# Experts' weights in 4 MB transfers from the eleventh expert on, normed tokens in the gathers' order, and memory products beside every second expert

## The reference

```python
def routed_experts(h, w_router, b_router, w_gate_up, b_gate_up, w_down, b_down):   # top 4 of 32
    ...
    def expert_block(args):
        xb, e = args
        gu = xb @ w_gate_up[e] + b_gate_up[e]          # (1024 x 2048)
        g, u = gu[:, :D_EXPERT], gu[:, D_EXPERT:]
        g = jnp.minimum(g, SWIGLU_LIMIT)
        u = jnp.clip(u, -SWIGLU_LIMIT, SWIGLU_LIMIT)
        glu = g * jax.nn.sigmoid(SWIGLU_ALPHA * g)
        return ((u + 1.0) * glu) @ w_down[e] + b_down[e]   # (1024 x 1024)
```

## Time and profile before

| | |
|---|---|
| median of three runs | 1755.46 us |
| the profiled execution: time, span | 1756.94 us, 1755.1 us |
| busy share PE, PEld, DVE, ACT, POOL | 93%, 59%, 40%, 33%, 1% |
| moved from HBM | 544 MB, mean 311 GB/s over the span |
| chain that ended last | PE 48%, DMA 31% (w_down 28%, w_gate_up 2%) |
| L948, gate_up's matmuls | 2000 records, 445.2 us busy |
| L989, down's matmuls | 992 records, 228.2 us busy |
| issues of w_gate_up, w_down | 125 and 61 of 2048 KB, 22.1 and 21.3 us to landing |
| issues of mem_w_kv | 8 of 1024 KB, 16.9 us to landing |

### The profile page before, as it was taken

One profiled execution on the slowest core, in us unless ns is written; L12 is line 12 of the kernel. 1 busy time (PEld: TensorE's weight loads), 2 busy tenths in 40 slices (PEclk: granted clock), 3 DMA queues, 4 the chain that ended last, 5 costly groups with the idle time before them and its releaser, 6 DMA issues.

```text
span 1755.1 us, 20263 instructions
## 1 busy us (share of the span) xinstructions
PE 1638.5 (93%) x8849; PEld 1033.2 (59%) x8850; DVE 705.3 (40%) x875; ACT 572.7 (33%) x787; POOL 22.5 (1%) x37
## 2 busy tenths in 40 slices
PE   8999999798889999998888888899999999999998
PEld 7788533333334444532323232378888998988886
DVE  5897412111111211211111111177664865567653
ACT  6576200111011111100000011176554765455552
POOL 0000000000000000000000000010000000000000
PEclk9999899999999999999999999999999999999999
DMA  7538999999999999999999999956555523445552
GB/s 246 174 101 307 382 427 428 427 427 427 427 428 426 428 427 427 427 427 427 429 428 428 427 426 427 408 169 208 188 191 174 170 97 126 165 135 187 191 192 96
DMA packets 118763, 546.39 MB, mean 311 GB/s; under 512 B 5697, under 2 KB 64193, under 8 KB 92977
## 3 DMA queue, kind: packets, MB, share of 16 engines
q1 hardware_dynamic: 117344, 540.96, 77.4%
q0 software_dynamic: 1040, 4.00, 0.8%
q10 hardware_dynamic: 288, 0.11, 0.0%
HBM read 544.00 MB, written 1.05 MB: 311 GB/s over the span
## 4 chain that ended last, share of the span: by engine, by line
PE 48%; DMA 31%; ACT 1%; DVE 1%; issue 0%; DVEq 0%; ACTq 0%
DMA ring<-in_w_down 28%; PE PS L624 8%; PE PS L989 8%; PE PS L1146 6%; PE PS L626 4%; PE PS L948 3%; DMA ring<-in_w_gate_up 2%; PE PS L609 1%; PE PS L610 1%; PE PS L611 1%; PE PS L1161 1%; DMA ring<-in_w_ple_gate 1%; PE PS L576 1%; PE PS L578 1%; PE PS L577 1%; PE PS L662 1%
## 5 line engine op out<-in xcount | busy, mean ns | idle before, releaser
L948 PE MATMUL PS<-ring,work 128*64 128x512 f32 x2000 | 445.2, 597 | 32.6 <-DMA ring<-in_w_gate_up 32.6
L1967 DVE TENSOR_TENSOR ring<-ring,ring 128x2048 fp32r<-128x2048 f32 (+2 forms) x130 | 289.3, 2234 | 258.6 <-ACT ring L1388 258.5
L948 PEld LDWEIGHTS PS<-ring,work 128*64 128x64 f32 x2000 | 138.8, 137 | 319.2 <-issue 246.9
L1388 ACT CAST ring<-ring 128x2048 fp32r<-128x2048 f32 (+2 forms) x131 | 243.2, 1869 | 211.4 <-DMA ring<-in_mem_w_kv 85.4
L989 PE MATMUL PS<-ring,work 128*64 128x512 f32 x992 | 228.2, 603 | 53.3 <-DMA ring<-in_w_down 40.4
L989 PEld LDWEIGHTS PS<-ring,work 128*64 128x64 f32 x992 | 71.9, 138 | 195.7 <-issue 152.5
L2399 DVE TENSOR_SCALAR work<-PS 128x512 f32<-128x512 f32 x32 | 22.1, 690 | 319.6 <-PE PS L948 319.6
L1643 ACT ACTIVATE work<-work 128x512 f32<-128x512 f32 x32 | 20.2, 631 | 361.0 <-DVE work L2399 361.0
L2295 DVE TENSOR_TENSOR work<-PS,work 128x512 fp32r<-128x512 f32 x32 | 22.1, 692 | 248.8 <-ACT work L1587 248.8
L624 PE MATMUL PS<-work,ring 128*128 128x512 f32 x320 | 111.2, 392 | 0.0
L624 PE MATMUL PS<-ring 128*128 128x512 f32 x320 | 111.2, 394 | 0.0
(11 more groups left out here) (437 smaller groups left out, 2332.9 us busy)
## 6 DMA issues: line engine op xcount, KB each, us to landing
ring<-in_w_gate_up SPq DMA_DIRECT2D x125, 2048.0 KB, 22.1
ring<-in_w_down SPq DMA_DIRECT2D x61, 2048.0 KB, 21.3
ring<-in_ffn_w_gu SPq DMA_DIRECT2D x44, 1024.0 KB, 5.1
ring<-in_w_in SPq DMA_DIRECT2D x28, 1024.0 KB, 5.5
ring<-in_ffn_w_down SPq DMA_DIRECT2D x22, 1024.0 KB, 4.7
ring<-in_w_out SPq DMA_DIRECT2D x8, 1024.0 KB, 5.1
ring<-in_mem_w_kv SPq DMA_DIRECT2D x8, 1024.0 KB, 16.9
work<-in_w_gate_up SPq DMA_DIRECT2D x2, 2048.0 KB, 18.7
```

What stands on the lines that cost most here:

```text
L948: t = e.matmul(PS[hf * 64:hf * 64 + 64, bank, :], XG[g % 2][:, 2 * kp + kk, i * 64:(i + 1) * 64], raw_chunk(w, kk)[:, c0 + hf * 512:c0 + h ...
L1388: e.copy(hi(j), raw(j)).then_inc(*act.now(("hi", j)))
L1967: e.tensor_tensor(lo(j), raw(j), hi(j).bitcast(F32), ALU.subtract).then_inc(*dve.now(("lo", j)))
```

## The change

The experts' two matrices may be joined from expert 10 on (up to 29): two parts in one transfer of 4 MB into two neighbouring slots. For that the two parts must be neighbours in memory on each partition: with rows `(p k)`, four rows of w_gate_up per partition in each half (32 KB) and all eight of w_down (32 KB); a single part takes two or four of them. The features of the tokens follow: `hnh` and `hnl` are written in the order in which the gathers read them, by reading x with a stride of four, so that a gather's weights are contiguous; `g_ffn_pairs` is permuted on the host. The hidden values follow as well: each half of the array now takes four of eight hidden columns in turn (`hidden`), for the weights and for the biases. The memory products move from experts 11 to 18 to every second one from 11 to 25, the transpose of p from 26 to 27, POOL's loads of p and the masks from group 5 to group 7. ACT's norm of the memory vectors also waits for DVE's `crowded`. The branch `spilled` follows the new row order.

```diff
--- before.py
+++ after.py
@@ -88,10 +88,10 @@
 PACKED = ("mem_w_kv_2", "w_ple_proj")
 X, Y, APART = NS, NS + 1, NS + 2
 CHECK = 6
-JOINED, FIRST_JOINED = (), 99
+JOINED, FIRST_JOINED = ('w_gate_up', 'w_down'), 10
 MEM_T = (6, 7, 9, 10)
-MEM_KV = tuple(range(11, 19))
-P_T, PLE_PROJ = 26, (28, 29, 30, 31)
+MEM_KV = tuple(range(11, 27, 2))
+P_T, PLE_PROJ = 27, (28, 29, 30, 31)
 
 
 class Plan:
@@ -118,7 +118,7 @@
             if e < NE:
                 add(("gate_up", e), [("w_gate_up", 2 * k, 2, 0, 2048) for k in range(4)], e, False)
             if e in MEM_KV:
-                add(("beside", e), [("mem_w_kv_2", 0, 8, (e - MEM_KV[0]) * 256, 256)])
+                add(("beside", e), [("mem_w_kv_2", 0, 8, MEM_KV.index(e) * 256, 256)])
             if e in PLE_PROJ:
                 add(("beside", e), [("w_ple_proj", 0, 2, (e - PLE_PROJ[0]) * 256, 256)])
             if e:
@@ -422,6 +422,11 @@
         hT32 = W(18240, 8, 256)
         hnl, hnh, rn = R32(0, 2, D), R32(2048, 2, D), ss_of["out"]
         XG = [W(4096, 8, 256), W(6144, 8, 256)]
+
+        def by_rows(v):
+
+            return v.rearrange("p (a q k) -> p a k q", a=2, k=4)
+
         PGr, PGr4 = R32(8192, 2, 256), R32(8192, 2, 4, 64)
         PGb = [B16(8704 + 512 * i, 2, 4, 128) for i in range(2)]
         PW = [R32(9728 + 256 * i, 256) for i in range(2)]
@@ -859,12 +864,15 @@
                 t = logits(k)
             t.then_inc(*pe.now("logits"))
 
+            def hidden(v, hf):
+                return v.rearrange("p (q z r) -> p q z r", z=2, r=4)[:, :, hf, :]
+
             def biases(n):
 
                 one_e = selb[0:96, n:n + 1].to_broadcast([96, 64])
                 for bank, c0 in ((bank_g(n), 0), (bank_u(n), DE)):
                     for hf in range(2):
-                        e.matmul(PS[hf * 64:hf * 64 + 64, bank, :], one_e, bgub[0:96, c0 + hf * 512:c0 + hf * 512 + 512],
+                        e.matmul(PS[hf * 64:hf * 64 + 64, bank, :], one_e, hidden(bgub[0:96, c0:c0 + DE], hf),
                                  start=True, stop=False, skip_group_check=True)
 
             for i in range(4):
@@ -887,7 +895,7 @@
                         if c == 0:
                             e.wait_ge(*dve["PG", g, h])
                         for z, half in enumerate((hnh, hnl)):
-                            t = e.matmul(PS[:, bank, c * 256:(c + 1) * 256], half[:, h, 256 * i + c:256 * i + 256:2],
+                            t = e.matmul(PS[:, bank, c * 256:(c + 1) * 256], half[:, h, 256 * i + c * 128:256 * i + c * 128 + 128],
                                          PGr[:, h, :], start=h == 0 and z == 0, stop=h == 1 and z == 1, skip_group_check=True)
                 t.then_inc(*pe.now(("gather", g, i)))
 
@@ -947,7 +955,7 @@
                             for hf in range(2):
                                 t = e.matmul(PS[hf * 64:hf * 64 + 64, bank, :],
                                              XG[g % 2][:, 2 * kp + kk, i * 64:(i + 1) * 64],
-                                             raw_chunk(w, kk)[:, c0 + hf * 512:c0 + hf * 512 + 512], start=False,
+                                             hidden(raw_chunk(w, kk)[:, c0:c0 + DE], hf), start=False,
                                              stop=kp == 3 and kk == 1, skip_group_check=True)
                     t.then_inc(*pe.now(("w", w), *([("gu", n)] if kp == 3 else [])))
 
@@ -1020,7 +1028,7 @@
                 e.wait_ge(o_bias, 16)
                 e.transpose(PS[:, 5, 0:16], obr, ident[0:16, 0:16]).then_inc(o_pe, 1)
                 for j in range(8):
-                    e.wait_ge(o_dma[j % 2], 32 * (j // 2 + 1))
+                    e.wait_ge(o_dma[j % 2], 64 * (j // 2 + 1))
                     e.wait_ge(o_v, 2 + 5 * j)
                     for i in range(2):
                         for k in range(8):
@@ -1029,7 +1037,7 @@
                     m.then_inc(o_pe, 1)
                 e.wait_ge(o_v, 2 + 5 * 8)
                 for j in range(4):
-                    e.wait_ge(o_dma[j % 2], 128 + 16 * (j // 2 + 1))
+                    e.wait_ge(o_dma[j % 2], 256 + 16 * (j // 2 + 1))
                     for kk in range(2):
                         for h in range(2):
                             for nb in range(2):
@@ -1571,7 +1579,8 @@
             x_chunks(2)
             e.wait_ge(*dve["factor_out"])
             for h in range(2):
-                e.activation(hnh[:, h, :], x[:, h, :], ACT.Identity, scale=rn[:, h:h + 1]).then_inc(*act.now(("hnh", h)))
+                e.activation(hnh[:, h, :].rearrange("p (a k q) -> p a k q", a=2, k=4), by_rows(x[:, h, :]), ACT.Identity,
+                             scale=rn[:, h:h + 1]).then_inc(*act.now(("hnh", h)))
             e.wait_ge(*dve["nmx"])
             for h in range(2):
                 e.activation(coef[:, h, :], lgx[:, h, 0:32], ACT.Exp, bias=nmx[:, h:h + 1]).then_inc(*act.now(("coef", h)))
@@ -1606,6 +1615,7 @@
             def memory_norm(h):
 
                 e.wait_ge(mem_in, 16 * (h + 1))
+                e.wait_ge(*dve["crowded"])
                 e.activation(mem_sq, mem, ACT.Square, accum_out=ss_of["mem_s"][:, h:h + 1]).then_inc(*act.now(("sq_mem_s", h)))
                 root("mem_s", h, ss_of["mem_s"])
 
@@ -1620,7 +1630,7 @@
                                          ACT.Identity, scale=gain("mem_kv_norm_2", k))
                     t.then_inc(*act.now(("beside", n)))
                 elif n in MEM_KV:
-                    c = n - MEM_KV[0]
+                    c = MEM_KV.index(n)
                     e.wait_ge(*pe["beside", n])
                     o = kT[:, 2 * c:2 * c + 2, :] if c < 4 else vm[:, :, (c - 4) * 256:(c - 3) * 256]
                     e.copy(o, PS[:, BM, :].rearrange("p (c t) -> p c t", c=2)).then_inc(*act.now(("beside", n)))
@@ -2245,9 +2255,11 @@
             def normed_rest(h, part):
 
                 c0, c1 = ((0, 256), (256, 512), (512, D))[part]
+                k0, k1 = ((0, 2), (2, 4), (0, 4))[part]
                 e.wait_ge(*act["hnh", h])
-                e.scalar_tensor_tensor(out=hnl[:, h, c0:c1], in0=x[:, h, c0:c1], scalar=rn[:, h:h + 1],
-                                       in1=hnh[:, h, c0:c1].bitcast(F32), op0=ALU.mult,
+                e.scalar_tensor_tensor(out=hnl[:, h, c0:c1].rearrange("p (k q) -> p k q", q=128),
+                                       in0=by_rows(x[:, h, :])[:, c0 // 512, k0:k1, :], scalar=rn[:, h:h + 1],
+                                       in1=hnh[:, h, c0:c1].bitcast(F32).rearrange("p (k q) -> p k q", q=128), op0=ALU.mult,
                                        op1=ALU.subtract).then_inc(*dve.now(("hnl", h, part)))
 
             normed_rest(0, 0)
@@ -2327,7 +2339,7 @@
                     e.wait_ge(o_turned, 1)
                     for c in range(8):
                         t = e.tensor_scalar(hT32[:, c, :], PS[:, 4 + c // 2, (c % 2) * 256:(c % 2) * 256 + 256],
-                                            gain("g_ffn", c), None, ALU.mult)
+                                            gain("g_ffn_pairs", c), None, ALU.mult)
                     t.then_inc(o_normed, 1)
                     with e.Fori(0, NE) as n:
                         m = e.value_load(cnt[0:1, bass.ds(n, 1)], min_val=0, max_val=S)
@@ -2795,7 +2807,7 @@
                     t = e.tensor_copy(PGb[g % 2][:, h, :, :].rearrange("p i (z s) -> p i z s", z=2),
                                       bc(PGr4[:, h, :, :].bitcast(F32), [128, 4, 2, 64], 2))
                 t.then_inc(*pool.now(("PGb", g)))
-                if g == 5:
+                if g == NE // 4 - 1:
                     e.wait_ge(*pe["beside", MEM_KV[-1]])
                     e.dma_start(p_raw, d["p"].rearrange("(h p) n -> p h n", p=128)).then_inc(p_in, 16)
                     e.dma_start(cst[:, C_HM:C_N], d["cst"][:, C_HM:C_N]).then_inc(hm_in, 16)
@@ -2825,9 +2837,10 @@
                     elif p.expert < 0:
                         src = rows(w, p.k0, p.k, p.c0, p.n)
                     elif p.name == "w_gate_up":
-                        src = w[p.expert][p.k0 * 128:(p.k0 + p.k) * 128, :].rearrange("(p k) n -> p k n", p=128)
+                        r0, k0 = p.k0 // 4 * 512, p.k0 % 4
+                        src = w[p.expert][r0:r0 + 512, :].rearrange("(p k) n -> p k n", p=128)[:, k0:k0 + n * p.k, :]
                     else:
-                        src = w[p.expert][p.k0 * 128:(p.k0 + p.k) * 128, :].rearrange("(p k) n -> p k n", p=128)
+                        src = w[p.expert].rearrange("(p k) n -> p k n", p=128)[:, p.k0:p.k0 + n * p.k, :]
                     if j == plan.apart:
                         e.wait_ge(*pe["merged_t", 3])
                         for kk in range(2):
@@ -2861,7 +2874,9 @@
                         e.wait_ge(o_pe, 1 + j - 1)
                     for i in range(2):
                         src = d["w_gate_up"][bass.ds(n, 1), :, i * DE + j * 128:i * DE + j * 128 + 128]
```

(6 more changed lines are left out.)

## The result

The changed kernel takes **1785.41 us** (median of 5 runs, 1780.68 to 1788.92) beside 1755.66 of the kernel before (5 runs, 1755.32 to 1760.34): a ratio of 1.0164, 95% interval 1.0153 to 1.0176. That is 29.8 us slower. I had forecast 18.5 slower, 1774.0, and a range up to 1781. The side and the mechanism were right. The size was not: the stream's start was priced too low, and losses that I had put at nothing were there. The profiled execution has a span of 1783.6 us, 28.5 more than before.

A forecast was written before the change was run, and what follows sets the result against it. The experts' in-order weight stream was taken to bound the kernel. Five gaps (23.7 us) less the joins' saving (5.5) plus the tokens' new order (0.3) made +18.5 on 1755.46: 1774.0 us, range 1754 to 1781.

The forecast's parts named there:

- the stream's start: Start and completion of a transfer issued into an empty stream: 2.1 us, 2.5 in the middle, from lone 1024 KB loads.
- What bounds: Experts' stage: the in-order weight stream decides, not the engines; a stretch in which it runs dry is lost for good.
- What a joined transfer saves: Weight stream: 0.107 us per 4096 KB transfer, 5.5 us for 51 joined ones (0 to 10.9).
- Rival B: Stream gaps as forecast, but a 4096 KB transfer saves nothing: dry 23.2 us, 1779.0 us; chance 11%.
- The setup-cost rule: Trainium skill: roughly fixed 2 us per transfer, 102 us for 51 if paid in the stream; forecast: full queue hides it.
- Where it goes dry: Loads of experts 14, 18, 20, 22, 26, whose second gate_up pair waits for memory weights' slots; nothing lost at 11, 15, 23.
- How large a gap is: Each dry place behind a memory product: 9.65 + 2.67 + 2.1 - 9.68 = 4.74 us, five are 23.7.
- The clock: PE idles about 5.3 us ahead of down, its clock falls to 0.50, down's first half takes 2.67 us more, all five places.
- Rival A: Gaps are there but the clock holds: 5 x 2.07 = 10.4 us, so 1760.7 us; chance 20%.
- The later stages: Everything after the experts' stage: unchanged, only later.
- The front: Normed tokens' strided reads on ACT and DVE before the experts' stream: 0.3 us, between 0 and 2.2.
- The sum: Whole kernel: 23.7 - 5.5 + 0.3 = +18.5 us, onto the median 1755.46: 1774.0 us; forecast's chance 42%.

The follow-up runs named there:

- experiment 1: Changed kernel with no joined transfers, everything else of the change kept: 1757.77 us, ratio 1.0006 to the kernel before.
- experiment 4: Changed kernel, both kinds joined, with PE making the memory product ahead of down's first half instead of between the halves: 1756.78 us, ratio 1.0000.
- experiment 2: Changed kernel with only w_gate_up joined (35 transfers), w_down as singles: 1756.07 us, ratio 0.9995.
- experiment 5: Changed kernel plus overwritten bf16 matmuls in PE's idle time ahead of down: 1781.52 us with 40 of them, 1780.30 us with 84.
- experiment 8: Changed kernel with the memory products beside experts 11 to 18 again, both kinds joined (55 joined loads): 1786.62 us, ratio 1.0164.
- the second run of experiment 5: Changed kernel plus a row of 84 overwritten bf16 matmuls, in place of 40, in PE's idle time ahead of down: 1780.30 us, ratio 1.0136.

## Where the prediction failed, and what it had right

In the span I forecast 18.5 us more, and it was 28.5. Two steps failed. The start of a stream that has stopped was priced at 2.1 us and took 3.1 on average. And everything outside five places behind memory products was put at nothing ("the whole after the experts' stage unchanged, only later"), but three more late loads cost 4.2, PE's late end 1.8 and a later stage 2.0. The saving was 1.9 too large on top of that. Smaller terms took 1.9 of all this back. Term by term:

- **What bounds**: right. The stream's dry time is the loss; experiment 1, with all but the joins, has none, and experiment 4, with all joins and no dry step behind a memory product, has no loss that can be measured.
- **What a joined transfer saves**: forecast 0.107, measured 0.07. In the changed kernel PE's waits for w_down end at 1002.67 and 1031.82, three joined transfers apart (section on the result), 29.15 us in place of 29.36. So 51 of them save 3.6 in place of 5.5. The size came from reading the memory load at 2.50; the landings say 2.48, and the same sum then gives 0.07. (The bound stands the wrong way round there: a 2.45 makes the saving 0.007, it is 2.55 that makes it 0.21.) Rival B (no saving at all) is out. In time experiment 2 shows 1.7 of 2.5. The setup-cost rule that I weighed there (the Trainium skill, SBUF — State Buffer, The DMA setup-cost knee) would by my estimate from its 2 us have given 102 us back. The full stream shows 0.07 per join, so it hides that cost; the stream begun anew shows it, at 2.4 us.
- **Where it goes dry**: right in all five places (14, 18, 20, 22, 26), and 11, 15, 23 lose nothing. Expert 16's single on the memory slot was missed: 1.7 us late, though issued 3.2 us before the stream ended. With a lead of 3.3 it was on time in experiment 5 (step 4.88), so this one isn't explained.
- **How large a gap is: a term too small.** I had 4.74 for each, from a release at 12.32 and 2.1 for start and completion. Measured over the five: release 11.78 on average, start and completion 3.1, a gap of 5.1, 25.7 in all and not 23.7. The 2.1 was the price of lone 1 MB loads. An undisturbed start of a 4 MB load costs 2.4, and three of the five were dearer (last section). I had seen 2.5 in the middle of those rows and put it only in the bounds. The starts cost 4.9 us more than I had, and the earlier releases took 2.7 of that back. That was luck: the clock's fall was shorter than forecast in four places and absent in one.
- **The clock**: a fall in four of the five, as forecast with 5.2 us of idle, but not in full: down's first half took 6.57, 6.40, 5.12, 3.65 (idle 3.50, no fall) and 6.47. Rival A (clock holds, 10.4 us) is out. With the clock held in experiment 5 the gaps at 14, 20 and 22 are 3.8, 1.9 and 4.0; its 2.07 fits the one with an undisturbed start.
- **What I left out**: the w_down loads for 28 and 29 wait for two slots of gate_up and are issued with only 2.5 and 2.6 us of stream before them (the first at 1079.35), and are 1.3 and 1.2 late (an instruction packet stands beside both, last section). I had looked for dry places only behind memory products. Behind the last load PE ends 1.8 us later than the stream does: it waits 3.44 ahead of down at 1124.15, and the fallen clock makes 5.35 of 3.65.
- **The later stages** took 607.6 in place of 605.5 us, though the change doesn't touch them. The 2.0 us are lost between 1225 and 1325, where PE gets through some 143 matmuls in 25 us in place of 146, at the same granted clock of 1.00. The trace of experiment 1, without a join, has the same loss at the same place, experiment 8's has it some 370 us later, and the second run of experiment 5 hasn't got it. So the joins don't make it; its cause stays open.
- **The front**: forecast 0.3. The load at the dry place goes out 0.5 later (217.01, before 216.51) but lands only 0.1 later (224.19, before 224.11). The strided reads are dearer than I had: ACT's scaling 2124 ns in place of 1144, which makes DVE's first remainder wait 1.80 instead of 0.82, and DVE's quarter ones 732 in place of 568. Nearly all is hidden. The Trainium skill (Advanced Engine Details and Errata, Memory Cachelines) asks for two hits on a 16-byte line: ACT's and DVE's reads have one and are slow, L956's operand has four and takes 604 ns, so the rows agree on both sides.
- **The sum** against the profiled execution: 0.1 + 27.4 - 3.6 + 2.5 = 26.4. The last gate_up lands 24.7 later than before (1143.58 against 1118.87), since single steps that are long in both kernels come to 1.7 less here. Then 1.8 and 2.0: 28.5.
- **The range** was too narrow above. Its top took my own bound of one gap, 5.14 each, which is what the five measured, and no saving, but nothing for places that I had not found (4.2 us), for PE's late end or for the later stages.

## What to carry to other kernels

When a queue of loads is what bounds a kernel, merging its transfers saves next to nothing (0.07 us for each pair here), but each merged one waits for two buffers and hands over both halves late. So count, for each load, how long before the end of the stream it can be issued, and keep that above what a start costs, here 2.4 to 4.9 us. If a consumer idles before late data while it still has work whose end frees a buffer, do that work first: this one move on PE was worth 29 us, where keeping the clock up was worth 5, and at most 12. And price a stall by the nearest row of the same size, with the disturbed cases in the range.

## What the runs showed that I had not expected

**A start into an empty stream has one price, and others on top of it.** In four kernels (the changed one, experiment 8 and both runs of experiment 5) 22 joined loads were issued less than 0.6 us before the stream's end or after it. Where no other queue moved anything between issue and landing, 12.1 or 12.2 us passed, in 8 of 8: 2.4 more than 9.72. Where one packet of instructions (q8) was fetched meanwhile, it was 13.3 to 13.8, in 10 of 10; with the other instruction queue's packet (q14) 12.9, once; with POOL's own transfers (q0, 0.39 to 0.45 MB) and an instruction packet or two 13.0 to 14.4, three times.

Packets of the changed kernel by queue, from 718.0 to 731.0, 848.7 to 862.0 and 977.6 to 990.4 (number, MB, share); between 784.1 and 796.0, with 12.1, there is q1 alone. These loads took 13.3, 13.4 and 13.0:

```profile
q8 instruction: 1, 0.02, 0.4%
...
q8 instruction: 1, 0.02, 0.5%
...
q0 software_dynamic: 112, 0.39, 7.5%
```

**The same in the full stream.** In the kernel before, 11 of 175 steps between 230 and 1080 us are over 0.3 us too long (packets counted from 1.8 us before one landing to 1.8 before the next). Three have 0.35 to 0.50 MB of q0 beside them and are 0.4 to 1.3 too long; eight have one instruction packet beside them and are 0.6 to 1.0 too long, in the changed kernel up to 1.4. None of the 139 steps with neither is long, but 25 with an instruction packet aren't either. In all eleven traces, from 440 us on, every such long step with neither beside it (up to 1140) belongs to a load that was issued less than 4.3 us ahead of the stream's end. So in a full stream the packet seems needed and not enough. That is a coincidence over many steps, not a tested cause: no run moved a fetch.

**A start is slow in its packets.** DMA share and GB/s of the changed kernel in 40 slices of 588 to 592 us:

```profile
DMA  0000000000099990000077000000707999700000
GB/s 0 0 0 0 0 0 0 0 0 0 0 2294 1311 328 655 0 0 0 0 0 328 328 0 0 0 0 0 0 328 0 328 1966 983 1311 328 0 0 0 0 0
```

The first packets come 0.9 us after the issue at 588.16, the second ones some 2 us after the first, while in the full stream they follow each other at about 1.2.

**The clock fell after less idle than before**: after 2.77 us in experiment 5, 2.09 in its second run, and 2.15 in the changed kernel at 1031.82, behind an ordinary gate_up (its row stands in the section on the result; a window as the earlier trace rows):

```profile
1032.00:1034.00 2.00, 2.00 (x6) 0.61 (x5) 0.58 (x1) 0.00 (x0) 0.00 (x0) 0.51 1.18 508
```

But 3.50 us at 839.18 left down's first half at 3.65, and so did 2.77 and 2.82 us at two places of experiment 5. The length of the idle time alone doesn't tell.
